# Rotary positions of one attention layer: the half-swap of rows done by DMA instead of by TensorE products

## The reference, cut to what matters

```
def _rotate(x, ang):
    cos = jnp.cos(ang)[None, :, None, :].astype(x.dtype)
    sin = jnp.sin(ang)[None, :, None, :].astype(x.dtype)
    x1, x2 = jnp.split(x, 2, axis=-1)
    return jnp.concatenate([x1 * cos - x2 * sin, x1 * sin + x2 * cos], axis=-1)
...
    q = axial_rope(rms_norm(q, q_gain), ang_row, ang_col)
    k = axial_rope(rms_norm(k, k_gain), ang_row, ang_col)
```

## Time and profile before

| | |
|---|---|
| median of 3 runs | 1526.22 us (1525.67 to 1526.79) |
| the profiled execution | 1526.18 us, of which the span of the profile is 1524.6 us |
| PE busy | 1510.4 us, 99% of the span |
| DVE, ACT, POOL busy | 938.5, 711.2, 76.2 us |
| chain that ended last | PE 98%, DMA 1% |
| DMA, hardware queue of SP | 49.3% of 16 engines' span |

### The profile page before, as it was taken

The page is one execution under the profiler, slowest core; times in us unless marked ns, Lnnn a source line. Parts: engine busy times, 40 slices in busy tenths (PEclk is TensorE's granted clock), DMA queues, the critical chain, the costliest instruction groups (busy, mean ns, idle before and its releaser), DMA issues.

```text
span 1524.6 us, 21609 instructions
## 1 busy us (share of the span) xinstructions
PE 1510.4 (99%) x9039; PEld 1260.0 (83%) x9039; DVE 938.5 (62%) x1234; ACT 711.2 (47%) x1002; POOL 76.2 (5%) x103
## 2 busy tenths in 40 slices
PE   7999999999999999999999999999999999999998
PEld 5777657778888888879778888899888899988887
DVE  6332585553424342466877667669789855779973
ACT  5411585342213222245764455545656546556553
POOL 0220041000000000000010000033000000000000
PEclk9999999999999999999999999999999999999999
DMA  9776424452532232453145555665555564565552
GB/s 359 239 206 222 121 32 168 164 194 85 191 111 83 85 108 90 158 194 111 56 166 177 184 188 171 220 201 194 175 197 181 194 193 150 182 203 170 195 191 83
DMA packets 244256, 251.38 MB, mean 165 GB/s; under 512 B 17229, under 2 KB 237744, under 8 KB 244160
## 3 DMA queue, kind: packets, MB, share of 16 engines
q1 hardware_dynamic: 242624, 247.48, 49.3%
q0 software_dynamic: 928, 1.87, 0.4%
q10 hardware_dynamic: 608, 0.66, 0.1%
HBM read 248.94 MB, written 1.05 MB: 164 GB/s over the span
## 4 chain that ended last, share of the span: by engine, by line
PE 98%; DMA 1%; DVE 0%; ACT 0%; issue 0%; SPq 0%; DVEq 0%; ACTq 0%
PE psum L394 95%; PE psum L995 3%; DMA vtok<-in_ctx 1%; PE psum L966 0%; PE psum L563 0%; ACT scr L674 0%; PE psum L2471 0%; DVE sums L1106 0%; ACT L680 0%; PE psum L2351 0%; DVE y L2517 0%; DVE scr L754 0%; DVE xl L745 0%; DVE pt L1128 0%; SPq L298 0%
## 5 line engine op out<-in xcount | busy, mean ns | idle before, releaser
L380 DVE TENSOR_TENSOR wl<-raw,wh 128x2048 fp32r<-128x2048 f32 (+1 forms) x183 | 413.6, 2262 | 251.6 <-ACT wh L373 251.4
L373 ACT ACTIVATE wh<-raw 128x2048 fp32r<-128x2048 f32 (+1 forms) x183 | 344.3, 1883 | 332.8 <-PE psum L394 285.3
L394 PE MATMUL psum<-x,wh 128*128 128x512 f32 (+1 forms) x1520 | 461.6, 364 | 0.0
L394 PE MATMUL psum<-x,wl 128*128 128x256 f32 x1312 | 367.5, 280 | 0.0
L394 PEld LDWEIGHTS psum<-x,wh 128*128 128x128 f32 x1520 | 271.7, 189 | 48.5 <-issue 1.4
L394 PEld LDWEIGHTS psum<-x,wl 128*128 128x128 f32 x1312 | 248.3, 189 | 0.0
L394 PE MATMUL psum<-xh,wh 128*128 128x512 f32 (+1 forms) x624 | 240.5, 385 | 0.3 <-DVE xl L745 0.3
L394 PE MATMUL psum<-xl,wh 128*128 128x512 f32 (+1 forms) x624 | 236.9, 380 | 0.0
L394 PE MATMUL psum<-xh,wl 128*128 128x512 f32 (+1 forms) x624 | 236.8, 380 | 0.0
L394 PEld LDWEIGHTS psum<-xh,wh 128*128 128x128 f32 x624 | 118.1, 189 | 29.4 <-DVE xl L586 4.3
L394 PEld LDWEIGHTS psum<-xh,wl 128*128 128x128 f32 x624 | 118.0, 189 | 22.0
(11 more groups left out here) (290 smaller groups left out, 1990.4 us busy)
## 6 DMA issues: line engine op xcount, KB each, us to landing
raw<-in_ffn_w_in SPq DMA_DIRECT2D x44, 1024.0 KB, 5.0
pre<-in_ada_w SPq DMA_DIRECT2D x27, 1024.0 KB, 9.7
raw<-in_w_ffn_gate SPq DMA_DIRECT2D x22, 1024.0 KB, 5.0
raw<-in_w_ffn_up SPq DMA_DIRECT2D x22, 1024.0 KB, 5.0
raw<-in_ada_w SPq DMA_DIRECT2D x21, 1024.0 KB, 5.4
raw<-in_w_ffn_down SPq DMA_DIRECT2D x19, 1024.0 KB, 4.7
raw<-in_ffn_w_out SPq DMA_DIRECT2D x16, 1024.0 KB, 4.6
raw<-in_na_w_qkv SPq DMA_DIRECT2D x10, 1024.0 KB, 6.6
```

The source lines that it names most:

```text
L373: act.e.activation(wh[:, c % NSPL, 0:z], raw[:, p % NRAW, 0:z], ACT.Copy).then_inc(W.hi, 1)
L380: dve.e.tensor_tensor(wl[:, c % NSPL, 0:z], raw[:, p % NRAW, 0:z], wh[:, c % NSPL, 0:z].bitcast(F32), ALU.subtract).then_inc(W.lo, 1)
L394: return pe.e.matmul(o, l, r, start=start, stop=stop, skip_group_check=shared)
```

## The change

The sign matrix `rot` and the six products with it are gone. SP copies rows within SBUF instead: in every group of 32 partitions, partitions 0 to 15 receive rows 16 to 31 and the reverse, so one tile takes eight transfers of 16 partitions. The sign is put into the sine table. The keys take 16 transfers of 16 KB (256 positions), each of the four query chunks 8 transfers of 32 KB. The swapped copies lie in `q_rot` (three buffers) and `k_rot` in SBUF, and DVE reads them there instead of in PSUM. The sine product of query chunk 3 moves from the end of the projections' stage to step 5 of the attention. The transfers stand in SP's list ahead of the loads of chunks 7, 8, 9 and of the first chunk after them.

```diff
-C_ID, C_ONE, C_EPS, C_BD, C_ROT, C_COS, C_SIN, C_CNT = 0, 128, 129, 130, 258, 386, 642, 898
-NCONST = 962
+C_ID, C_ONE, C_EPS, C_BD, C_COS, C_SIN, C_CNT = 0, 128, 129, 130, 258, 514, 770
+NCONST = 834
...
-        c[d, C_SIN:C_SIN + T] = np.sin(a)
+        c[d, C_SIN:C_SIN + T] = np.sin(a) * (-1.0 if d % 32 < 16 else 1.0)
...
+        q_rot, k_rot = at(94, "q_rot", [P, 3, TT]), at(100, "k_rot", [P, 2, T])
...
+            def rotate(to, t, done):
+                for x in range(0, P, 32):
+                    sp.e.dma_start(to[x:x + 16, :], t[x + 16:x + 32, :]).then_inc(done, 16)
+                    sp.e.dma_start(to[x + 16:x + 32, :], t[x:x + 16, :]).then_inc(done, 16)
+
+            def rotate_query(i):
+                sp.wait_ge(R1.copy, i + 1)
+                if i:
+                    sp.wait_ge(R1.rot, 128 * i)
+                if i == 3:
+                    sp.wait_ge(X1.free, AUX_Q[0] + 1)
+                rotate(q_rot[:, i % 3, :], slot(q_cp[i]), R1.rot)
+
...
+                if (kind, x) == ("w", first_o1 + 1):
+                    rotate_query(0)
+                elif (kind, x) == ("w", first_o1 + 2):
+                    sp.wait_ge(X1.free, 2)
+                    for m in range(2):
+                        rotate(k_rot[:, m, :], slot(k_cp[m])[:, 0:T], K1.rot)
+                    rotate_query(1)
+                elif (kind, x) == ("w", first_o1 + 3):
+                    rotate_query(2)
+                elif (kind, x) == ("w", first_o1 + 4):
+                    rotate_query(3)
...
-                u = AUX_Q[i]
-                aux_free(u)
-                pe.wait_ge(R1.copy, i + 1)
-                mm(aux[u][:, :], rot, slot(q_cp[i]), True, True).then_inc(R1.rot, 1)
...
-                elif i == 2:
-                    for m in range(2):
-                        aux_free(AUX_KROT[m])
-                        pe.wait_ge(X1.free, m + 1)
-                        mm(aux[AUX_KROT[m]][:, 0:T], rot, slot(k_cp[m])[:, 0:T], True, True).then_inc(K1.rot, 1)
...
+        def query_sin(i):
+            dve.wait_ge(R1.rot, 128 * (i + 1))
+            dve.wait_ge(R1.cos, i + 1)
+            dve.e.tensor_tensor(two(slot(q_cp[i])), two(q_rot[:, i % 3, :]), sin.unsqueeze(1).to_broadcast([P, 2, T]),
+                                ALU.mult).then_inc(X1.free, 1)
...
-                dve.wait_ge(R1.rot, i + 1)
-                dve.wait_ge(R1.cos, i + 1)
-                dve.e.tensor_tensor(two(q), two(x), tab[1], ALU.mult).then_inc(X1.free, 1)
                 if i < 3:
+                    query_sin(i)
                     query_sum(i)
...
-                        s, q, x = slot(k_sq[m]), slot(k_cp[m]), aux[AUX_KROT[m]]
+                        s, q, x = slot(k_sq[m]), slot(k_cp[m]), k_rot[:, m, :]
...
-                        dve.wait_ge(K1.rot, m + 1)
+                        dve.wait_ge(K1.rot, 256)
...
                 elif i == 1:
-                    pe.wait_ge(X1.free, AUX_Q[2] + 1)
+                    pe.wait_ge(X1.free, 2)
                     pe.wait_ge(R1.root, 1)
                 elif i == 2:
-                    pe.wait_ge(X1.free, AUX_Q[3] + 1)
                     pe.wait_ge(R1.copy, 4)
...
+                elif i == 5:
+                    query_sin(3)
                 elif i == 6:
                     query_sum(3)
```

More of the change, by code:

```diff
@@ L45, in shape_constants @@
     c[:, C_BD:C_BD + P] = (i[:, None] // 64 == i[None, :] // 64)
[L46 to L50, removed]
     t = np.arange(T)
@@ L177, in program @@
         bd = cst[:, C_BD:C_BD + P]
-        rot = cst[:, C_ROT:C_ROT + P]
         cos = cst[:, C_COS:C_COS + T]
@@ L1415, in program @@
         kbank, qbank, vbank = bank[1:3], [bank[3], bank[4], bank[5], bank[1]], bank[4:6]
-        aux = [bank[(6, 0)[u % 2]] for u in range(8)]
+        aux = [bank[6], bank[0]]
         AUX_K, AUX_KROT, AUX_Q = (0, 1), (3, 4), (2, 5, 6, 7)
@@ L1423, in program @@
         q_sq, q_cp, q_out = (8, 10, 12, 0), (9, 11, 9, 1), (8, 10, 3, 0)
-        def aux_free(u):
-            if u >= 2:
-                pe.wait_ge(X1.free, u - 1)
         def qkv1_pe():
@@ L1546, in query_turn @@
             def query_turn(i):
-                s, q, x = slot(q_sq[i]), slot(q_cp[i]), aux[AUX_Q[i]]
-                tab = [t.unsqueeze(1).to_broadcast([P, 2, T]) for t in (cos, sin)]
+                s, q = slot(q_sq[i]), slot(q_cp[i])
                 dve.wait_ge(R1.copy, i + 1)
                 dve.wait_ge(R1.stat, i + 1)
-                dve.e.tensor_tensor(two(s), two(q), tab[0], ALU.mult).then_inc(R1.cos, 1)
-                dve.wait_ge(R1.rot, i + 1)
-                dve.wait_ge(R1.cos, i + 1)
-                dve.e.tensor_tensor(two(q), two(x), tab[1], ALU.mult).then_inc(X1.free, 1)
+                dve.e.tensor_tensor(two(s), two(q), cos.unsqueeze(1).to_broadcast([P, 2, T]), ALU.mult).then_inc(R1.cos, 1)
                 if i < 3:
+                    query_sin(i)
                     query_sum(i)
```

## The result

| kernel | median of its runs | ratio to before, 95% interval |
|---|---|---|
| before | 1526.22 us (11 runs) | |
| changed | 1529.57 us (11 runs, 1528.66 to 1531.03) | 1.0026 [1.0018, 1.0034] |

The change makes the kernel 3.35 us slower by the medians, some 4 us by the ratio of the table; the interval excludes no change. My forecast was 1525.3 us, no measurable change. The time is inside the range, just under its upper end of 1529.6, and close to the 1529.3 us of the rival with dear issues; the direction that I forecast was wrong.

The account below looks back on a forecast made before the run. PE was taken to bound the kernel (98% of the chain), DVE close behind. DVE's smaller gain, 2.0 - d = 1.0 us, less 0.1 for the moved sine product, gave 1526.18 - 0.9 = 1525.3 us; range 1523.2 to 1529.6.

Parts of the forecast that it names:

- the rival with dear issues: Key transfers on SP: each issue costs 0.66 us like the bias loads, d = +5.0, 1529.3 us; chance 0.18.
- the price of an issue: SP's 16 key transfers: 0.40 us each, from the store of y at 0.358 plus some 0.04 between issues.
- d: Delay of DVE's first sine product of the keys, waiting for all 16 transfers, against its old start: +1.0 us.
- The products' price: Swap products leaving PE in layer 1's projections, 0.9 us at each of five places: 4.5 us, bounds 4.3 and 5.2.
- The gap on PE: PE stands still ahead of the sums of squares of query chunk 2, for 1.2 + d: 2.2 us.
- DVE's bound of 2.0 - d - 0.1: Gain DVE's order allows up to the scores of step 3, 1.0 us, less 0.1 for the moved sine product.
- The query transfers and delayed weight loads at nothing: Query chunks' swapped rows land before DVE wants them; delayed weight loads have some 60 us of cover: no cost.
- The moved sine product nearly free in step 5: Query chunk 3's sine product in attention step 5, where DVE waits 0.43 us for PE: about 0.1 us reaches PE.
- the clock's fall: PE's clock falls in the new 2.2 us gap: 1.7 us lost, 0.3 to 0.7 showing, 1525.8 us; chance 0.10.
- PE's bound of 3.3 - d: Gain PE's order allows: 4.5 us of products less the standstill of 1.2 + d, leaving 2.3 us.
- The rival of free issues: Key transfers on SP: issues cost nearly nothing, rows land before DVE asks, all 4.5 us kept, 1521.8 us; chance 0.10.
- transfers land one after the other: Key transfers: 16 landings of 2.1 us in sequence, 34 us, kernel slower by over 25 us; chance 0.04.

Follow-up runs that it names:

- no_swap: Changed kernel with neither swap transfers nor products, the sine products reading unswapped rows: 1521.28 us against 1525.43 of before, ratio 0.9974.
- warm: Changed kernel with twenty unused 128x512 products in PE's gap ahead of query chunk 2's sums of squares: 1527.82 us against 1525.43 of before, ratio 1.0014.
- keys11: Changed kernel with 11 key transfers instead of 16, and by a slip chunk 96 loaded in place of chunk 8: 1526.68 us against 1525.49 of before.
- keys_pe: Changed kernel with the keys' swap back on PE as a product, the queries' swap still by SP: 1521.64 us against 1525.49 of before, ratio 0.9976.
- keys4x2: Changed kernel with eight key transfers carrying both tiles, four issued by SP and four by ACT: 1521.5 us against 1525.49 of before, ratio 0.9974.
- keys11c: Changed kernel with 11 key transfers instead of 16, chunk 8 loaded correctly: 1526.36 us against 1525.12 of before, ratio 1.0005.
- queues2: Changed kernel with the 16 key transfers issued from two lists, tile 0 by SP, tile 1 by ACT: 1523.31 us against 1525.43 of before, ratio 0.9987.
- keys8: Changed kernel with both key tiles in one transfer, eight of 32 KB instead of sixteen of 16 KB: 1523.38 us against 1525.43 of before, ratio 0.9982.
- keys11_warm2: Changed kernel with 11 key transfers and nine unused 128x512 products in PE's gap: 1524.23 us against 1525.12 of before, ratio 0.9996.

## Why the prediction was wrong

**The step that failed: the price of an issue.** The prediction said "That gives 0.40 us per transfer", from the store of y at 0.358 us. It was 0.63: 0.59 and a gap of 0.04. Two things were missed. First, this kind of transfer is dearer even behind a wait: the first key issue took 0.51 us and the first of query chunk 0 0.59, where the store of y and the weight loads take 0.36 and 0.37. Second, a transfer directly behind a burst costs more than alone: the later key issues took 0.59 us, and in the changed kernel the load of chunk 7, 0.37 us alone at 701.76, takes 0.52 directly behind eight transfers (timeline of SP).

```profile
701.91 0.59 SPq L308 DMA_DIRECT2D q_rot<-scr  x1
702.60 0.52 SPq L379 DMA_DIRECT2D raw<-in_gqa_w_o  x1
```

The trace of before had this already, in a row that I did not use (SP's timeline, before): the same kind of load took 0.37 us alone and 0.62 directly behind the bias loads.

```profile
78.49 0.37 SPq L360 DMA_DIRECT2D raw<-in_na_w_qkv  x1
...
89.84 0.62 SPq L360 DMA_DIRECT2D raw<-in_na_w_qkv  x1
```

The rows of small transfers in a burst were these bias loads. I named them, gave the reason "many short pieces" against them, and took the lone store instead. I also misread them: 12 times 0.626 is 7.5 us and not 10.89. Only six of the twelve took 0.63; the other six took 0.88 to 1.41, so their starts lie 0.91 apart on average. The gap of 0.04 holds all the same.

In the sum for d, the last key issue started 9.85 us after the first, not 6.0: 3.85 us too little. SP started 0.2 us earlier than I took, and the landing was 0.3 shorter (1.8 us, not 2.1), so d came out 3.3 us too small. The landing is also under the 2.04 us that the Trainium skill's fit gives (DMA: Bandwidth & Descriptors, section Anatomy of one DMA); that fit is for transfers issued by GpSimd, and these were issued by SP.

**The steps that held.** The products' price, 4.5 us with a little taken back: no_swap gains 4.15. The gap on PE, 1.2 + d = 5.5 us: measured 5.28. DVE's bound of 2.0 - d - 0.1: -2.4 worked out, -2.0 in the profile of warm. With the landing where I had it and the clock held, keys11's profile gives 738.60 for the scores of step 3, forecast 738.9, and the stage's own gain is 1.0. The query transfers and delayed weight loads at nothing: keys_pe. The moved sine product nearly free in step 5: keys4x2 ends where no_swap does.

**The rivals.** The one with issues as dear as the bias loads was the case that came: d = +5.0 and 1529.3 us forecast, +4.3 and 1529.57 measured. That its time came so close is luck in part, for it was made by two costs where the rival had one: with d = +4.3 DVE's bound alone gives a loss of 2.4 us, and the rest is the clock. **This is the second step that failed:** the clock's fall had no term in the sum. I held it for a separate case at 1.7 us with room of 1 to 1.4 us to hide in. It came with the gap of 5.28 us and with one of the two gaps of 2.2. In the changed kernel it lengthened the tiny products by 0.9 us and 26 weight products by 0.09 each, 3.3 us on PE, and 2.4 of them passed through to step 3. PE's bound of 3.3 - d less these 3.3 is -4.3, and the profile shows -4.4. Even my own forecast case needed that term: at a gap of 2.2 us the clock falls in some executions and not in others, and keys11c's median is 1.2 us above before rather than 0.9 under it. The rival of free issues is excluded on one list. The Trainium skill calls issue time usually small beside the transfer (DMA: Bandwidth & Descriptors, section Issuing engines are not separate DMA queues); here one issue took 0.59 us of the 1.8 to landing, and sixteen took 10 us for 256 KB in all. The same section says that issuing from several engines saves the sequencer's time, and queues2 shows that in numbers: the last issue starts at 710.7 instead of 715.8. That transfers land one after the other is excluded by the landing of 1.8 us at issues 0.63 apart: several were under way at once.

What stays open: why an issue of these transfers takes 0.5 to 0.6 us and that of a weight load 0.37; why a few issues take much longer; and why the clock at 696 to 700 held in more executions of keys_pe.

## What to carry to other kernels

Count transfers, not bytes: a burst of n small transfers on one list lands n times its issue time later, and the price must be read from a row where issues stand directly behind each other. Fold tiles into one transfer and share the burst between two lists before giving up on it; with four transfers on each of two lists this change gains 4.0 us instead of losing 3.35. When a change opens a gap on TensorE, price the gap twice: the gap itself, and the products behind it at half the clock. At the gap of 2.2 us here half of the executions paid that second price, by their mean granted clock.

## What the runs showed of the hardware

- Issues of DMA from SP: 0.59 us and a gap of 0.04 for 16 rows of 1 KB, for 16 rows with two pieces of 1 KB, and about the same for 112 rows of 2 KB. A weight load of 1 MB takes 0.37 us alone; directly behind such a burst it took 0.52 or 0.53 in three cases of the changed kernel and 1.71 in the fourth. Single issues within a burst are long too: 0.81 us for the third key issue of the changed kernel, 1.92 for one query issue of keys4x2.
- ACT issued the same transfers at 0.62 us each while SP issued its own at 0.59, as it does alone. In keys4x2, with 32 KB each, ACT's four took 0.81 us in the median.
- In the gap of 5.28 us the granted clock fell at about 721, with PE still idle, and PE ran at the lower of its two levels until about 731. With gaps of 2.15 and 2.16 us it held the clock in one profile and lost it in the other, there at about 721.7, just behind PE's restart at 721.31. With gaps of 0.5 to 0.8 us (keys8, queues2, warm, keys11_warm2) it held in every profile here.
- The clock can fall without any gap: at 696 to 700, behind tiny products, the granted clock is 0.57 in the profile of before and 1.00 in that of keys_pe.
